# The second mixer, computed one token block at a time inside the expert slots

## The reference, cut to what matters

```
for i in range(2):
    h = rms_norm(x, norm_mix_g[i])
    y = mla_mixer(h, ...) if i == 0 else fox_mixer(h, ...)
    x = x + y
    h = rms_norm(x, norm_ffn_g[i])
    x = x + peer_ffn(h, peer_w_q[i], peer_sub_keys[i], peer_u[i], peer_v[i])
```

```
a   = gelu(einsum('tkd,td->tk', u[idx], x)) * g
out = einsum('tk,tkd->td', a, v[idx])
```

## Time and profile before

| | us |
|---|---|
| median of the timed executions | 3809.72 |
| span of the profiled execution | 3811.5 |
| TensorE matmul busy | 3089.0 (81%) |
| VectorE busy | 1726.9 (45%) |
| GpSimd busy | 1697.6 (45%) |
| ScalarE busy | 1009.5 (26%) |
| bytes moved, mean rate | 1242.05 MB, 326 GB/s |
| mean granted TensorE clock | 0.919 |

### The profile page before, as it was taken

One profiled execution on the slowest core, in us unless ns is written; L12 is line 12 of the kernel. 1 busy time (PEld: TensorE's weight loads), 2 busy tenths in 40 slices (PEclk: granted clock), 3 DMA queues, 4 the chain that ended last, 5 costly groups with the idle time before them and its releaser, 6 DMA issues.

```text
span 3811.5 us, 33124 instructions
## 1 busy us (share of the span) xinstructions
PE 3089.0 (81%) x9272; PEld 1715.4 (45%) x9272; DVE 1726.9 (45%) x3093; ACT 1009.5 (26%) x2401; POOL 1697.6 (45%) x1145
## 2 busy tenths in 40 slices
PE   7888788888867777777699998788888877777777
PEld 6445644444423322222577876644444433222232
DVE  3333255555545555555311121255555555555554
ACT  3334322222212222221144443222222222222221
POOL 4003455444434444444177665455444444444443
PEclk8877999999988999999699998899999999999999
DMA  4113599999999999999178683599999999999998
GB/s 156 58 58 118 173 417 416 417 417 417 407 415 390 405 413 410 410 411 414 48 170 163 158 147 122 199 417 416 417 417 417 408 387 411 409 411 408 411 406 367
DMA packets 253041, 1242.05 MB, mean 326 GB/s; under 512 B 25888, under 2 KB 63264, under 8 KB 120864
## 3 DMA queue, kind: packets, MB, share of 16 engines
q0 software_dynamic: 147456, 1073.81, 68.3%
q1 hardware_dynamic: 105504, 167.23, 15.9%
HBM read 1238.85 MB, written 2.10 MB: 326 GB/s over the span
## 4 chain that ended last, share of the span: by engine, by line
PE 29%; DMA 28%; issue 23%; DVE 9%; POOL 9%; ACT 2%; SPq 0%; POOLq 0%; DVEq 0%; ACTq 0%
DMA room<-in_peer_u_dram,index 26%; PE psum L906 18%; POOL w_low L545 6%; PE psum L840 3%; POOL room L566 2%; PE psum L628 2%; PE psum L629 2%; PE psum L630 2%; DVE room L1671 2%; DMA room<-in_peer_v_dram,index 1%; ACT diag L1236 1%; POOL room L561 1%; DVE work L1646 1%; DVE work L1650 1%; DVE key_f L1652 1%
## 5 line engine op out<-in xcount | busy, mean ns | idle before, releaser
L906 PE MATMUL psum<-room,diag 128*128 128x512 f32 x4096 | 1939.4, 623 | 593.5 <-ACT diag L1236 584.2
L1671 DVE CUSTOM_DVE_ANT_0 room<-room,normed 128x2048 f32<-128x2048 f32 x512 | 1186.0, 2325 | 1195.0 <-DMA room<-in_peer_u_dram,index 1194.0
L906 PEld LDWEIGHTS psum<-room,diag 128*128 128x128 f32 x4096 | 789.5, 199 | 1667.5 <-issue 947.5
L566 POOL DMA_INDIRECT room<-in_peer_v_dram,index x512 | 571.2, 1116 | 1111.3 <-PE psum L906 560.9
L561 POOL DMA_INDIRECT room<-in_peer_u_dram,index x512 | 643.4, 1257 | 420.0 <-DVE dots L1671 191.2
L545 POOL TENSOR_TENSOR w_low<-wbuf,w_high 128x2048 fp32r<-128x2048 f32 (+1 forms) x108 | 480.8, 4462 | 556.5 <-ACT w_high L982 556.4
L1227 ACT ACTIVATE acts<-dots 128x1 f32<-128x1 f32 x512 | 103.8, 203 | 1903.2 <-DVE dots L1671 1903.2
L982 ACT ACTIVATE w_high<-wbuf 128x2048 fp32r<-128x2048 f32 (+1 forms) x108 | 200.4, 1859 | 279.7 <-DMA wbuf<-in_fox_w_in_dram 142.3
L628 PE MATMUL psum<-w_high,x_high 128*128 128x512 f32 (+1 forms) x608 | 242.5, 399 | 4.3 <-POOL w_low L545 4.3
L629 PE MATMUL psum<-w_low,x_high 128*128 128x512 f32 (+1 forms) x608 | 237.9, 391 | 0.0
L630 PE MATMUL psum<-w_high,other 128*128 128x512 f32 (+1 forms) x608 | 237.9, 391 | 0.0
(11 more groups left out here) (164 smaller groups left out, 1939.6 us busy)
## 6 DMA issues: line engine op xcount, KB each, us to landing
wbuf<-in_fox_w_in_dram SPq DMA_DIRECT2D x64, 1024.0 KB, 7.7
wbuf<-in_peer_w_q_dram SPq DMA_DIRECT2D x64, 512.0 KB, 15.5
wbuf<-in_mla_w_o_dram SPq DMA_DIRECT2D x16, 1024.0 KB, 5.1
wbuf<-in_fox_w_o_dram SPq DMA_DIRECT2D x16, 1024.0 KB, 5.1
wbuf<-in_mla_w_in_dram SPq DMA_DIRECT2D x8, 1024.0 KB, 8.2
wbuf<-in_mla_w_kvb_dram SPq DMA_DIRECT2D x32, 256.0 KB, 3.3
room<-in_peer_u_dram,index POOLq DMA_INDIRECT x512, 15.4
room<-in_peer_v_dram,index POOLq DMA_INDIRECT x512, 14.3
```

Of the source, the lines that this page charges most:

```text
L566: pool.indirect_dma_start(v_ring[:, r, :], None, peer_v.rearrange("l n d -> (l n) d"), bass.IndirectOffsetOnAxis(index[:, p, s:s + 1], 0)) ...
L906: mm = pe.matmul(psum[:, 4 * b + q, :], diag[:, r, :], v_ring[:, r, q * TILE:(q + 1) * TILE], start=False, stop=False, skip_group_check=True)
L1671: V.tensor_tensor_reduce(u_ring[:, r, :], u_ring[:, r, :], normed[:, b, :], 1.0, 0.0, ALU.mult, ALU.add, dots[:, r:r + 1]).then_inc(dot_do ...
```

## The change: what it does

1. The fox mixer no longer has a stage of its own. Its work for block 0 is cut into pieces that the engines execute between the slots of window 1, and its work for block 1 between those of window 2 (`job(b, at)` on each engine, `at` being the slot's number in its window). Block 0's keys and values are kept in SBUF (`past_kT`, `past_v`) for block 1.
2. A job consists of the norm (slots 1 to 4), the forget logits (6 to 9), 16 tiles of `fox_w_in` at one quarter a slot (slots 6 to 69) with attention trailing them, 16 quarters of `fox_w_o` (slots 70 to 78 and 83 to 89), the second norm (91 to 95), and layer 1's queries for this block (16 quarters of `peer_w_q`, slots 96 to 111) with their scores, which are kept.
3. The weights are read once per block, so twice, into a ring of four 1 MB stages (`stage`, 98 loads a job) that SP refills when TensorE has used one. `peer_w_q[1]` is now read in rows of 2 KB instead of 1 KB.
4. These products are plain float32 matmuls: no `w_high` and `w_low`, no work on ScalarE and GpSimd for them.
5. In every slot TensorE now takes three matmuls (1536 columns), and VectorE adds the last 512 columns of v, scaled, directly to `resid` (`axpy`), one slot later.
6. GpSimd issues the gather of u one slot ahead of that of v (`LEAD = 1`).
7. `choose` is cut in three parts, after slots 9, 10 and 11. All slots are written out; the hardware loops over the units are gone.

```diff
-CHOOSE_AT = 11
+CHOOSE_AT = 10
+LEAD = 1
+PE_BANKS = 3
+PE_COLS = PE_BANKS * TILE
+STAGES = 4
+MIX_AT = 1
+IN_AT = 6
+GROUP = 16
+HEAD_AT = 14
+OUT_AT = IN_AT + 4 * GROUP
+LAST_OUT_AT = 83
+FFN_AT = 91
+PQ_AT = 96
@@ SyncE
+            def stage_quarter(job, m, w, q, c0):
+                r = staged(job, m)          # waits for stage_used of the load four before
+                sp.dma_start(stage[:, r], w[:, 4 * q:4 * q + 4, c0:c0 + TILE]).then_inc(stage_full[r], 16)
+            for job in range(NB):
+                stage_gain(job, M_MIX, norm_mix_g[1:2, :])
+                for g in range(4):
+                    for t in range(4):
+                        for q in range(4):
+                            stage_quarter(job, M_IN + 16 * g + 4 * t + q, fw, q, t * D + g * TILE)
+                for m, (t, q) in enumerate(OUT_ORDER):
+                    stage_quarter(job, M_OUT + m, ow, q, t * TILE)
+                stage_gain(job, M_FFN, norm_ffn_g[1:2, :])
                 for t in range(4):
-                    load_quarters(S_FOX + t, 2 * g, fw, bass.ds(g * TILE + t * D, TILE))
-            after_attention(fox, norm_ffn_g[1:2, :])
+                    for q in range(4):
+                        stage_quarter(job, M_PQ + 4 * t + q, qw, q, t * TILE)
@@ GpSimd
+            for n in range(LEAD):
+                gather_u(n)
+            for n in range(slots):
+                if n + LEAD < slots:
+                    gather_u(n + LEAD)      # waits for dot n-3
+                gather_v(n)                 # waits for the matmuls and the axpy of n-4
@@ TensorE
+                for q in range(PE_BANKS):
+                    mm = pe.matmul(psum[:, q, :], diag[:, r, :], v_ring[:, r, q * TILE:(q + 1) * TILE],
+                                   start=at == 0, stop=at == WINDOW - 1, skip_group_check=True)
+            def gemm_quarter(job, m, q, bank, src):
+                r, turn = stage_of(job, m)
+                pe.wait_ge(stage_full[r], 16 * (turn + 1))
+                for c in range(4):
+                    k = 4 * q + c
+                    last = pe.matmul(psum[:, bank, :], src[:, k, :], stage[:, r, c, :], start=k == 0, stop=k == KC - 1)
+                last.then_inc(stage_used, 1)
@@ VectorE
+            def axpy(n):
+                V.scalar_tensor_tensor(out=resid[:, b, PE_COLS:D], in0=v_ring[:, r, PE_COLS:D],
+                                       scalar=acts[:, 1, r:r + 1], in1=resid[:, b, PE_COLS:D],
+                                       op0=ALU.mult, op1=ALU.add).then_inc(axpy_done, 1)
+                for n in range(UNITS * SLOTS):
+                    dot(n)
+                    if n:
+                        axpy(n - 1)
+                    if at == 0 and n:
+                        close(window - 1)
+                    if CHOOSE_AT - 1 <= s < CHOOSE_AT + 2 and number + 1 < UNITS:
+                        choose(number + 1, s - CHOOSE_AT + 1)
+                    if window in (1, 2):
+                        job(window - 1, at)
```

More of the change, by code:

```diff
@@ L470, in _ @@
                     load_tile(half, number, quarters(half, w, bass.ds(g * n, n), n))
[L472 to L480, removed]
-                n0, w = W_PQ[at.layer], rows_view(peer_w_q[at.layer])
-                with sp.Fori(0, PHEADS // 2) as i:
-                    for t in range(2):
-                        half = (n0 + t) % 2
-                        load_tile(half, (n0 + t) // 2 + i,
-                                  quarters(half, w, bass.ds(i * 4 * P + t * 2 * P, 2 * P), 2 * P))
@@ L489, in _ @@
[L489 to L492 removed]
+            halves_used(W_PQ0)
+            w = rows_view(mla_w_o[0])
+            with sp.Fori(0, 2) as i:
+                for t in range(2):
+                    load_quarters(S_O0 + t, i, w, bass.ds(i * 2 * TILE + t * TILE, TILE))
+            mla.ot_done.done(sp, mla.groups - 1, mla.ot_done.n - 1)
+            load_gains(1, norm_ffn_g[0:1, :])
+            all_used(S_O0 + 3)
@@ L497, in _, with staged, stage_gain @@
-            sp.wait_ge(peer_added, NB)
-            load_gains(2, norm_mix_g[1:2, :])
-            for t in range(1, 4):
-                load_quarters(S_FOX + t, 0, fw, slice(t * D, t * D + TILE))
-            with sp.Fori(1, fox.groups) as g:
+            sp.wait_ge(queried, PHEADS - 1)
+            def staged(job, m):
+                n = LOADS * job + m
+                if n >= STAGES:
+                    sp.wait_ge(stage_used, n - STAGES + 1)
+                return n % STAGES
+            def stage_gain(job, m, g):
+                r = staged(job, m)
+                sp.dma_start(stage[:, r].rearrange("p c n -> p (c n)"),
+                             g.broadcast_to([P, D])).then_inc(stage_full[r], 16)
@@ L570, in _ @@
                 low_parts([S_IN + t], width)
-            for layer in range(2):
-                if layer:
-                    low_parts_looped(S_FOX, 4 * fox.groups)
-                low_parts_looped(S_O[layer], 4)
-                with pool.Fori(0, NB * PHEADS // 2) as i:
-                    for p in range(2):
-                        gathers(layer, layer * NB * PHEADS + 2 * i + p, p)
+            low_parts_looped(S_O0, 4)
+            slots = UNITS * SLOTS
+            for n in range(LEAD):
+                gather_u(n)
```

1042 lines of the change are left out of this document (649 added, 393 removed).

## The result

The changed kernel takes 3723.84 us (median of four executions, 3715.82 to 3724.76), beside 3809.89 us for the kernel before in the same runs. The ratio is 0.9771, with a 95% interval from 0.9757 to 0.9785, so it is 86 us faster. 3740 us was forecast, with a range of 3640 to 3850. The profiled execution has a span of 3722.3 us.

A forecast was written before the change was run, and what follows sets the result against it. DMA engines were taken to bound the PEER windows. Start 467.8, first dot 8.8, windows 679.5, 967, 955 and 636, bubbles 13 and end 13 summed to 3740 us; range 3640 to 3850 us.

The forecast's parts named there:

- 616 us of stage and some 50 us of pauses: Fox stage and pauses between a layer's windows: both go, traded for some 600 us of DMA time.
- DMA-bound through (case 1): Whole kernel: DMA engines bound it, odd groups at 4.3 us a quarter; 3740 us, own range 3695 to 3800, chance 0.45.
- Cheap quarters at 2.94 us: Windows 1 and 2: each quarter of even `fox_w_in` groups, `fox_w_o` and `peer_w_q` costs 2.94 us of DMA time.
- Dear quarters at 4.3 us: Windows 1 and 2: each quarter of `fox_w_in` groups 1 and 3 costs 4.3 us, between 2.94 and 5.68.
- 3653 and 3892 us: Whole kernel: every quarter at 2.94 us gives 3653 (chance 0.24); quarters keeping their prices alone give 3892 (chance 0.13).
- 331 us of loads a job: Windows 1 and 2: DMA time of a job's 96 weight quarters and two gains, 94 + 138 + 94 + 5 us.
- 13 us of bubbles: Windows 1 and 2: 0.7% of their time added for waits coupling the engines, 13 us.
- TensorE hidden at 6.9 and 7.3 us a slot: Busy slots of windows 1 and 2: TensorE's work stays under the DMA time, 1.1 to 1.5 us to spare.
- case 4: Windows 1 and 2: TensorE's order of work bounds, 8.9 us a busy slot, 1013 us a job's window; 3844 us, chance 0.12.
- Window 0 at 688 us: Window 0: 636 us of plain slots plus 43.5 us of q1, 679.5, with 8.8 us to the first dot.
- Axpy, lead, `choose` in three: Windows 0 and 3: these edits change nothing that ends last; priced at the plain 636 us.

The follow-up runs named there:

- even: The changed kernel with the `fox_w_in` quarters of groups 1 and 3 read from the columns of groups 0 and 2: 3629.71 us, ratio 0.9535.
- odd: The changed kernel with the `fox_w_in` quarters of groups 0 and 2 read from the columns of groups 1 and 3: 3805.85 us, ratio 0.9989.
- wide: The changed kernel with `fox_w_in` loaded as 2 chunks by 1024 columns, rows of 4 KB, each load serving two groups: 3617.31 us, ratio 0.9493.
- small: The changed kernel with each weight quarter of a job but the first four loading only 128 of 512 columns, products computed in full: 3396.51 us, ratio 0.892.
- mm4: The changed kernel with a fourth matmul of 512 columns in every slot, one bank added twice: 3725.07 us, ratio 0.9774.
- lead0: The changed kernel with the gather of u issued in the same slot as that of v (`LEAD = 0`): 3718.98 us, ratio 0.976.
- choose1: The changed kernel with `choose` in one piece after slot 11 instead of three parts: 3727.46 us, ratio 0.9789.
- wide4: `wide` with a fourth matmul of 512 columns in every slot, one bank added twice: 3614.04 us, ratio 0.9483.

## Why the prediction was right, step by step

Its mechanism was a trade: 616 us of stage and some 50 us of pauses against the DMA time of the loads, laid on windows that DMA bounds. The windows of both kernels bear it out. The stage's 616.5 us are gone; windows 1 and 2 grew by 284.4 and 245.7 us (671.9 to 956.3, 702.0 to 947.7); the rest is 3 us. That makes the 89 us between the two spans. The parts, predicted (a start of 467.8 us, the first dot and the bubbles shared out) and measured:

| | predicted | measured |
|---|---|---|
| first gather | 467.8 | 469.5 |
| window 0 | 688 | 702.6 |
| window 1 | 973 | 956.3 |
| window 2 | 962 | 947.7 |
| window 3 with the end | 649 | 646.2 |
| span | 3740 | 3722.3 |

- **DMA-bound through (case 1).** Right. `even`, `odd` and `wide` move the time by what they change of q1's time, and TensorE, made heavier, moves nothing; only `small` gains less than q1's share loses.
- **Cheap quarters at 2.94 us.** Right: 2.94 and 3.03 (the last 7 us of group 2's stretch, at 165 to 175 GB/s, are already group 3's). Those of `fox_w_o` and `peer_w_q` were a little cheaper, 2.81 us (30.0% of 1760 to 1860 us for 11.21 MB) and 2.75 (25.4% of 1870 to 1960 us for 8.72 MB).
- **Dear quarters at 4.3 us.** A choice of the middle between 2.94 and 5.68, and right: 4.25 and 4.11 by the queue's share. No row spoke for the middle, so that it was hit so well is luck; `even` and `odd` put the difference at 1.39 us, so 4.3. Whether they stay dear was the whole doubt between 3653 and 3892 us; from the trace of before alone it couldn't be settled, since no row showed one among gathers. The thought that random gathers between them weaken the collision agrees with 5.68 and 5.90 us in the stage against 4.3 among gathers, and with the 3.84 us of dear and cheap pieces in turn, but the mechanism itself wasn't shown.
- **331 us of loads a job.** 320 measured in window 1, and 32.3% of 947.7 = 306 in window 2, where 319 were counted. About 5 us of each difference are the cheaper `fox_w_o` and `peer_w_q`.
- **13 us of bubbles.** Too much, as far as it can be read: window 1 is 636 + 320 with nothing left over, window 2 636 + 306 and 6 more, and the subtraction itself is good to 10 or 20 us. `choose`, whose waits count in this term, costs 4 us at most in one piece.
- **TensorE hidden at 6.9 and 7.3 us a slot (against case 4).** Right. `small` shows it near its bound, at a granted clock of 0.97: 781 and 796 us a window, where 96 x 6.9 + 32 x about 3 = 758 and 96 x 7.3 + 96 = 797 would be the sums. Case 4's 1013 us was far off: the order of work is loose enough for waits of up to 18 us to be caught up by dots in a row.
- **Window 0 at 688 us** is the term that was mis-sized, by 14 us. About 5 us are the place of the cut: the measured window ends at the dot of slot 1 of the next one (1172.00 us), so it holds a slot more than 128, and window 3 one less. About 6 us are q1: 7.0% of 702.6 us = 49 us, where 43.5 were counted. The last 3 or 4 are missing in `even` and `odd`, whose window 0 is the same program and takes 698.8 us. The kernel before needed 701.8 us for the same window, cut in the same way, and that was the row to take. The gathers aren't to blame: q0's 94.2% for 273.79 MB, or 261 gathers, are 2.53 us each, beside 2.52 in plain slots.
- **Axpy, lead, `choose` in three.** Priced at nothing in windows 0 and 3, rightly; each by itself is worth nothing that can be measured elsewhere either (`mm4`, `lead0`, `choose1`).

The sum came out 18 us too high, from -17 and -14 in windows 1 and 2, -3 in window 3, and +16 up to the end of window 0: errors of both signs, so a part of the small difference is luck too.

## What to carry to other kernels

When one stage is bound by DMA and another by compute, laying the second between the first's slots is worth the second stage's time less the DMA time of what it must load again; price each kind of load from the queue's own busy share, not from its bytes, and among the traffic that it will meet: the dear quarters cost 5.7 us in the stage and 4.3 among gathers. Where the same shape of load takes different times at different columns, try another row length first: here rows of 4 KB instead of 2 KB brought 107 us, more than the whole restructuring. Long waits between engines in a trace say nothing against an order of work as long as the bounding resource stays full.

## What the runs showed of the hardware

- Loads of 2 KB rows at a pitch of 32,832 bytes, with nothing else moving, take 3.5 to 6.3 us per 1.05 MB by their start column; at exactly 32 KiB, and at 32,896 bytes, 2.8 us.
- Among gathers of 8 KB rows the dear ones take 4.3 us of the DMA engines' time, the cheap ones 2.94, rows of 4 KB 2.62.
- Loads added to a stretch that the DMA engines already filled added their own busy time: 633 to 648 us were left in eight windows of four kernels without q1's share, beside 636 us for 128 plain slots.
- One core moved 420 to 422 GB/s through the plain slots, and `wide` 407 and 411 over the whole of windows 2 and 1, with their loads.
- The granted TensorE clock was higher with more work: 0.889 over the change's span, 0.953 with a fourth matmul a slot (0.906 and 0.959 for `wide` and `wide4`), and TensorE's added 203 us of busy time cost no time of the kernel.
